# The attention output product of layer 2 as one level of Strassen, and the weight copies moved into layer 1's attention

## The reference

```
h  = rms_norm(x, norm_g);  u = h @ w_in
v_c, b_c, c_c, z_c, q, k, v, z_a, gate_logits = split(u)
y_c = b_c * causal_depthwise_conv(c_c * v_c, conv_w) * silu(z_c);   y_a = y_c @ w_conv_out
o   = sliding_window_attention(rms(q), rms(k), v, sinks) * silu(z_a);  y_b = o @ w_attn_out
g_a, g_b = split(sigmoid(gate_logits + gate_b))
out = x + (g_a * y_a + g_b * y_b) @ w_out
```

## Time and profile before

| | |
|---|---|
| median of three runs | 816.91 us |
| the profiled execution | 816.7 us |
| its span | 814.7 us |
| PE (matmul) busy | 99% |
| PEld (weight load) busy | 84% |
| DVE busy | 75% |
| ACT busy | 40% |
| POOL busy | 22% |
| piece 88, first of the attention output product, starts | 604.61 us |
| the gate stage starts | 691.65 us |

### The profile page before, as it was taken

How to read it: one execution, slowest core, us unless ns; L and a number is a source line. 1 busy time by engine, 2 the same in 40 slices (tenths; PEclk the granted TensorE clock), 3 DMA queues, 4 the chain that set the end, 5 groups by cost and what they waited for, 6 DMA issues and landing times.

```text
span 814.7 us, 11429 instructions
## 1 busy us (share of the span) xinstructions
PE 808.5 (99%) x4220; PEld 687.1 (84%) x4220; DVE 609.4 (75%) x1096; ACT 321.9 (40%) x701; POOL 182.6 (22%) x189
## 2 busy tenths in 40 slices
PE   9999999999999999999999999999999999999998
PEld 7778888888888888888888888888888888999986
DVE  4998778768984476885579788978952269599998
ACT  4374465632212255334445554441000122355580
POOL 2212111111111221121324445444323224000000
PEclk9999999999999999999999999999999999999999
DMA  7332214445143222653365555566876335866562
GB/s 239 87 97 77 79 52 153 158 157 179 53 155 126 82 83 77 208 175 90 91 130 130 125 119 120 128 130 155 168 165 158 104 88 145 233 182 183 182 205 78
DMA packets 129565, 108.92 MB, mean 134 GB/s; under 512 B 4525, under 2 KB 101350, under 8 KB 129510
## 3 DMA queue, kind: packets, MB, share of 16 engines
q1 hardware_dynamic: 123142, 95.60, 38.4%
q0 software_dynamic: 6336, 12.58, 9.4%
q10 hardware_dynamic: 32, 0.01, 0.0%
HBM read 106.08 MB, written 27.26 MB: 164 GB/s over the span
## 4 chain that ended last, share of the span: by engine, by line
PE 92%; DVE 5%; issue 1%; ACT 1%; DVEq 0%; ACTq 0%
PE proj L1736 24%; PE proj L1738 24%; PE proj L1737 24%; PE bank_t L1750 3%; PE bank_o L1825 2%; DVE x L1447 1%; DVE w_lo L1142 1%; PE score L1738 1%; PE score L1737 1%; PE score L1736 1%; PE score L1900 1%; PE score L1899 1%; PE score L1811 1%; PE score L1810 1%; PE bank_o L1918 1%
## 5 line engine op out<-in xcount | busy, mean ns | idle before, releaser
L723 POOL TENSOR_SCALAR w_hi<-w_raw 128x1024 fp32r<-128x1024 f32 x109 | 128.8, 1182 | 436.2 <-DMA w_raw<-in_w_in_dram 310.8
L1142 DVE TENSOR_TENSOR w_lo<-w_raw,w_hi 128x1024 fp32r<-128x1024 f32 x145 | 179.9, 1244 | 60.2 <-POOL w_hi L723 59.6
L1736 PE MATMUL proj<-xt_hi,w_hi 128*128 128x512 f32 (+1 forms) x448 | 171.1, 382 | 0.0
L1738 PE MATMUL proj<-xt_hi,w_lo 128*128 128x512 f32 (+1 forms) x448 | 168.1, 375 | 0.0
L1737 PE MATMUL proj<-xt_lo,w_hi 128*128 128x512 f32 (+1 forms) x448 | 167.8, 375 | 0.0
L1738 PEld LDWEIGHTS proj<-xt_hi,w_lo 128*128 128x128 f32 x448 | 84.4, 188 | 15.5
L1737 PEld LDWEIGHTS proj<-xt_lo,w_hi 128*128 128x128 f32 x448 | 84.5, 189 | 14.2
L1736 PEld LDWEIGHTS proj<-xt_hi,w_hi 128*128 128x128 f32 x448 | 84.5, 189 | 13.9
L1736 PE MATMUL proj<-w_hi,xt_hi 128*128 128x512 f32 x152 | 61.0, 401 | 0.2 <-ACT prob L922 0.2
L1738 PE MATMUL proj<-w_hi,xt_lo 128*128 128x512 f32 x152 | 59.5, 392 | 0.0
L1737 PE MATMUL proj<-w_lo,xt_hi 128*128 128x512 f32 x152 | 59.4, 391 | 0.0
(11 more groups left out here) (420 smaller groups left out, 1774.4 us busy)
## 6 DMA issues: line engine op xcount, KB each, us to landing
w_raw<-in_w_in_dram SPq DMA_DIRECT2D x79, 512.0 KB, 3.8
w_sums<-in_w_in_dram SPq DMA_DIRECT2D x8, 1024.0 KB, 7.5
w_raw<-w_sums SPq DMA_DIRECT2D x32, 256.0 KB, 3.3
w_raw<-in_w_out_dram SPq DMA_DIRECT2D x14, 512.0 KB, 3.3
w_raw<-in_w_in_dram SPq DMA_DIRECT2D x26, 256.0 KB, 3.6
w_sums<-w_sums POOLq DMA_DIRECT2D x6, 1024.0 KB, 9.9
w_sums<-in_w_out_dram SPq DMA_DIRECT2D x4, 1024.0 KB, 6.8
w_sums<-in_w_in_dram POOLq DMA_DIRECT2D x4, 1024.0 KB, 9.9
```

The lines of the kernel that those rows point to most:

```text
L723: pool.tensor_scalar(hi, raw, 1.0, 1.0, ALU.mult, ALU.mult).then_inc(hi_done, 1)
L1142: dve.tensor_tensor(lo, raw, hi.bitcast(F32), ALU.subtract).then_inc(w_split, 1)
L1736: pe.matmul(out, left[0], right[0], start=first, stop=False)
L1738: return pe.matmul(out, left[1], right[0], start=False, stop=last)
```

## The change

1. The attention output product becomes one level of Strassen in 14 pieces (`AOUT` = 88 to 101, `COUT` = 102 the first of the convolution's output product): seven block products for each of two column pairs. A piece is a weight block's 512 rows x 256 columns, 2 x 4 x 3 = 24 matmuls of 256 tokens, still in the ring of 4 slots.
2. A fourth group of `w_sums` (four copies, four gathers more). The 16 copies stand behind the loads of pieces 12 to 27; the 16 gathers at pieces 53, 55, 57, 59, 62, 64, 66, 68, 71, 73, 75, 77, 80, 82, 84, 86, the new group first. POOL waits for a group's copies, not for all.
3. `OS`: ACT rounds, DVE takes the low part, and for half of the chunks only 256 tokens. The factor 0.5 of the results moves into the gating (0.5 becomes 0.25).
4. Four sums of activations on DVE at pieces 85 to 87, rounded on ACT at 87 and 88, low parts on DVE at 88, 88, 89, 90. Results are combined on DVE (`combine_out`), for each pair seven additions of 512 numbers, in place of ACT's eight tiles.
5. The banks rotate over all eight; the first pieces behind wait for the last additions.

```diff
-U_AOUT = U_CONV + KC
-U_COUT = U_AOUT + KC // 4
+U_COUT = U_CONV + KC
+AOUT = 4 * U_COUT
+OUT_PIECES = 7 * 2
+COUT = AOUT + OUT_PIECES
+GATES = 4 * UNITS + OUT_PIECES
+OUT_ORDER = [A11, A12, A22, S2, S1, S4, S3]
+GROUPS = 4
+ATTENDED = 3
-COPY_AT = [*range(4 * U_GA, 4 * U_O0), *range(4 * U_Z0, 4 * U_Z1)]
-SUM_AT = [4 * U_Z1 + 4 + 3 * i for i in range(4 * GROUPS)]
+COPY_AT = range(4 * U_RQK, 4 * U_O0)
+GROUP_ORDER = [ATTENDED, 0, 1, 2]
+SUM_AT = [4 * U_Z1 + 1 + 9 * i // 4 for i in range(4 * GROUPS)]
+SO_SUM_AT = ((AOUT - 3, 1), (AOUT - 2, 0), (AOUT - 2, 1), (AOUT - 1, 0))
+SO_HI_AT = ((AOUT - 1, 0), (AOUT - 1, 1), (AOUT, 0), (AOUT, 1))
+SO_LOW_AT = ((AOUT, 0), (AOUT, 1), (AOUT + 1, 1), (AOUT + 2, 1))
...
+            if n < COUT:
+                pair, i = divmod(n - AOUT, 7)
+                return [right_of(ATTENDED, OUT_ORDER[i])[:, 256 * pair:256 * pair + 256].rearrange("(k p) c -> p k c", p=P)]
...
+        def out_bank(x):
+            return gate_banks[(x + SLOTS) % 8]
...
+                if n == AOUT:
+                    sp.wait_ge(w_gathered[ATTENDED], 16 * 4)
...
-                group, step = divmod(i, 4)
+                group, step = GROUP_ORDER[i // 4], i % 4
                 t = (0, 2, 1, 3)[step]
-                if i == 0:
-                    pool.wait_ge(w_copied, 16 * 4 * GROUPS)
+                if step == 0:
+                    pool.wait_ge(w_copied[group], 16 * 4)
                 if step >= 2:
                     pool.wait_ge(w_gathered[group], 16 * step)
...
+                        elif kind == "OS":
+                            act.wait_ge(o2_gated, WIN_STEPS)
+                            tokens = slice(0, 256 if m < 4 else S)
+                            act.activation(o2_hi[:, m, tokens], gT2[:, m, tokens], ACT.Copy).then_inc(o2_hi_done, 1)
...
+            def attended_sum(i):
+                x11, x12, x21, x22 = (quarter(gT2, row, col) for row in range(2) for col in range(2))
+                if i == 0:
+                    dve.wait_ge(o2_split, KC)
+                    dve.tensor_tensor(x22, x22, x21, ALU.subtract).then_inc(so_summed, 1)
...
+            def attended_low(i):
+                product = (S2, S1, S4, S3)[i]
+                dve.wait_ge(so_hi_done, i + 1)
+                hi, lo = sum_of_attended(product)
+                dve.tensor_tensor(lo, raw_sum(product), hi.bitcast(F32), ALU.subtract).then_inc(so_split, 1)
...
+            def combine_out(x):
+                pair, i = divmod(x, 7)
+                product = OUT_ORDER[i]
+                if product in (A11, A22):
+                    return
+                psum, kept = out_bank(x), out_bank(7 * pair + OUT_ORDER.index(A22))
+                dve.wait_ge(piece_done, AOUT + x + 1)
...
+                elif product == S3:
+                    dve.scalar_tensor_tensor(out=out(1, 1), in0=v_sum_out, scalar=-1.0, in1=psum, op0=ALU.mult, op1=ALU.subtract).then_inc(out_combined, 1)
+                    dve.tensor_tensor(w_sum, w_sum, psum, ALU.add).then_inc(out_combined, 1)
+                    dve.wait_ge(out_combined, 7 * pair + 6)
+                    dve.tensor_tensor(out(1, 0), w_sum, kept, ALU.add).then_inc(out_combined, 1)
...
+                    if half == 1 and AOUT <= n < COUT:
+                        combine_out(n - AOUT)
...
+            def attended_product(x):
+                n = AOUT + x
+                product = OUT_ORDER[x % 7]
+                wait_low(n)
...
+                else:
+                    wait_combined_out(x - 8)
+                if x < 7 and LEFT[product][0]:
+                    pe.wait_ge(so_split, (S2, S1, S4, S3).index(product) + 1)
+                left = left_of_attended(product)
+                w = [ring_parts(n, i)[0] for i in (1, 2)]
+                for j in range(2):
+                    for k in range(4):
+                        last = products(out_bank(x)[:, j, :], [t[:, k, j * P:(j + 1) * P] for t in w], [t[:, k, :] for t in left], k == 0, k == 3)
+                last.then_inc(piece_done, 1)
...
                         if u == U_COUT:
                             pe.wait_ge(yc_done, KC)
+                            wait_combined_out(8 + q)
```

More of the change, by code:

```diff
@@ L127, in unit_columns @@
             (TRA, [("w_in_2", Z2 + 512 + P * j) for j in range(4)])][u]
-    if u < U_AOUT:
+    if u < U_COUT:
         t = u - U_CONV
         return TRA, [("w_in_2", c + P * t) for c in (CV, CC, CB, CZ)]
-    t = 4 * ((u - U_AOUT) % (KC // 4))
-    return TRA, [("w_attn_out_2" if u < U_COUT else "w_conv_out_2", P * (t + j)) for j in range(4)]
+    return TRA, [("w_conv_out_2", P * (4 * (u - U_COUT) + j)) for j in range(4)]
 UNIT = [unit_columns(u) for u in range(UNITS)]
@@ L446, in left_of, with sum_of_attended, left_of_attended @@
             return [t[:, chunk:chunk + 4, token:token + 256] for t in ((hi, lo), (s_hi, s_lo))[source]]
+        def sum_of_attended(product):
+            place = {S2: 0, S1: 1, S4: 2}
+            if product == S3:
+                return [quarter(t, 1, 0) for t in (o2_hi, o2_lo)]
+            return [t[:, 4 * place[product]:4 * place[product] + 4, :] for t in (so_hi, so_lo)]
+        def left_of_attended(product):
+            source, chunk, token = LEFT[product]
+            if source:
+                return sum_of_attended(product)
+            return [t[:, chunk:chunk + 4, token:token + 256] for t in (o2_hi, o2_lo)]
         def pair_of(t, c, r):
@@ L846, in take_first, with take_first_out @@
                 act.activation(u_sum, gate_banks[7 * c % 8], ACT.Copy).then_inc(u_copied, 1)
+            def take_first_out(pair):
+                act.wait_ge(yc_done, KC)
+                if pair:
+                    act.wait_ge(out_combined, COMBINED[S2])
+                act.wait_ge(piece_done, AOUT + 7 * pair + 1)
+                act.activation(u_sum, out_bank(7 * pair), ACT.Copy).then_inc(out_first, 1)
             def take_tanh(c, r):
@@ L963, in _ @@
                         else:
[L965 to L968, removed]
+                            if u >= U_COUT:
+                                t = 4 * (u - U_COUT) + j
+                                act.wait_ge(out_combined, OUT_PIECES)
+                                act.activation(part[:, t, :], b, ACT.Copy, scale=0.5).then_inc(evacuated[j], 1)
                                 continue
-                            if u > U_CONV and last_tanh[0] < U_AOUT and last_tanh[0] >= U_CONV:
+                            if u > U_CONV and last_tanh[0] < U_COUT and last_tanh[0] >= U_CONV:
                                 act.wait_ge(yc_done, u - U_CONV)
@@ L983, in _ @@
                         gate_step(n - GATES)
-                    if half == 1 and 4 * U_COUT + 2 <= n < 4 * U_COUT + 6:
-                        q = n - 4 * U_COUT - 2
+                    if (n, half) in SO_HI_AT:
+                        product, after_sums = ((S2, 3), (S1, 1), (S4, 4), (S3, 2))[SO_HI_AT.index((n, half))]
+                        act.wait_ge(so_summed, after_sums)
+                        act.activation(sum_of_attended(product)[0], raw_sum(product), ACT.Copy).then_inc(so_hi_done, 1)
+                    if half == 1 and AOUT <= n < COUT:
+                        if (n - AOUT) % 7 == 0:
+                            take_first_out((n - AOUT) // 7)
+                    if half == 1 and COUT + 2 <= n < COUT + 6:
+                        q = n - COUT - 2
                         act.wait_ge(sx_summed, (4, 6, 8, 10)[q])
@@ L1691, in _ @@
                         left_lows(c)
-                    if half == 1 and 0 <= n - 4 * U_COUT < 5:
-                        input_sums(n - 4 * U_COUT)
-                    if half == 1 and 0 <= n - 4 * U_COUT - 3 < 4:
-                        input_low(n - 4 * U_COUT - 3)
+                    if half == 1 and AOUT <= n < COUT:
+                        combine_out(n - AOUT)
+                    if half == 1 and 0 <= n - COUT < 5:
+                        input_sums(n - COUT)
+                    if half == 1 and 0 <= n - COUT - 3 < 4:
+                        input_low(n - COUT - 3)
                     if n >= FINAL and (n - FINAL) % 2:
@@ L1717, in _ @@
                         take_tiles(n, half)
-                    if half == 1 and WIN_FIRST <= n < 4 * U_AOUT and not splits_wait(n, half):
+                    if half == 1 and WIN_FIRST <= n < AOUT and not splits_wait(n, half):
                         for m in ROUNDED_AT[n]:
                             split_piece(m)
+                    if (n, half) in SO_LOW_AT:
+                        attended_low(SO_LOW_AT.index((n, half)))
+                    if (n, half) in SO_SUM_AT:
+                        attended_sum(SO_SUM_AT.index((n, half)))
                     if (n, half) == (0, 0):
```

127 lines of the change are left out of this document (90 added, 37 removed).

## The result

The changed kernel takes 819.1 us (median; 817.9 to 821.0), the kernel before on the same chip 817.0 (816.2 to 817.8): ratio 1.0027, 95% interval 1.0019 to 1.0035, slower by 0.27%. The profiled run took 818.0 us, 1.3 more than the profiled run of before; its span of 816.2 is 1.57 us over the span of before.

What follows compares the result with a forecast made beforehand. PE, busy 808.5 of 814.7 us, was taken as the bound. -3.20 + 5.0 + 0.25 + 0.1 = +2.15 us on the profiled 816.7 gave 818.9, as the median 819.1 us; range 813.8 to 821.8.

Steps and rivals of the forecast that it cites:

- the second rival: Attention output product: the stall only eats the gain, stop 3.4 us, 817.5 us; with stops of 1.6 to 4.4, chance 0.27.
- the forecast: Likeliest case: a stop of 4.4 to 6 us in the attention output product, 818.5 to 820.2 us, chance 0.4.
- Term 1: Attention output product itself: 14 pieces of 2.88 us, 40.32 us instead of 43.52, a gain of 3.20 us.
- Term 3: Attention output product: weight loads held behind late accumulating copies make PE stand once, 5.0 us, before piece 92.
- the upper case: Attention output product: copies of 12.1 us each, or the load of piece 89 held too, give a 6.2 us stop.
- the forecast's own case: Load of piece 92, held behind the last accumulating copy, lands at 618.6 and stops PE for 5.0 us.
- Term 2: Four-slot weight ring at 2.88 us a piece: the shorter cover still suffices, cost 0, bounds 0 to 2 us.
- the sums of term 4: DVE's four activation sums before piece 90: cost 0 thanks to DVE's idle time; without it 4.9 us would delay piece 90.
- term 4: Small edges: piece 103's bank 0.25 us, copies behind pieces 12 to 27 0.1, moved rounding and window attention masks 0.
- The clock: Half clock behind the stall in the attention output product: counted as 0, with +2.9 us kept for the range.
- the first: Rival for the attention output product: loads are not held, PE never stands, 814.1 us, chance 0.2.

Runs made afterwards that it cites:

- e7: Kernel before with only the change's data movement (16 copies, 16 accumulating copies), its attention output product as it was: 817.3 us, ratio 0.9997.
- e9: Changed kernel with accumulating copies behind pieces 52, 54, ... 82 and DVE's four sums two to three half pieces earlier: 816.0 us, ratio 0.9985.
- e10: e9 with its last accumulating copy moved from behind piece 82 to behind piece 87: 819.3 us, ratio 1.0022.
- e5: Changed kernel with its 16 accumulating copies behind pieces 48, 50, ... 78: 819.3 us, ratio 1.0026.
- e6: e5 with DVE's four sums also two to three half pieces earlier: 818.8 us, ratio 1.0021.
- e12: e9 with ScalarE instead of POOL rounding weight pieces 91 to 101: 815.4 us, ratio 0.9979.
- e2: Changed kernel with only DVE's four sums moved two to three half pieces earlier: 818.9 us, ratio 1.0018.
- e4: Changed kernel with PE streaming 22 idle matmuls before it waits for the low half of piece 90: 818.7 us, ratio 1.0017.
- e8: e6 with six PE waits forced by ScalarE copies, before pieces 97 to 109; ran once, stops of 1.11 to 5.23 us, whole time not given.
- e11: e9 with ScalarE's casts and DVE's low halves of the four sums one half to two half pieces earlier: 817.1 us, ratio 1.0001.

## Why the prediction came out as it did

The median was forecast to the tenth (819.1) and the sign is right, but the tenth is luck: two wrong sizes cancelled, and the profiled run, forecast at 818.9, took 818.0. Half of the working is wrong. The sign that the prediction set itself, one stop of 4 to 6 us before the fourth or fifth product, was not met: the stop was 2.81 us, before the third. By its stop the run belongs to the second rival (1.6 to 4.4), by its time to the forecast.

- **Term 1 (-3.20): right.** 0.12 apart, 336 times, 40.32 us.
- **Term 3 (+5.0 at piece 92): right in kind, wrong in place, size and path.** A load held behind a late accumulating copy is at the head of PE's stop (e7, e9 and e10 show it from three sides). But it was the load of 89, which the text gave as the upper case, and it reached PE one piece later, through DVE's row: DVE waited for POOL's rounding at piece 89, and the stop before 90 came from the order of DVE's program. The stop was 2.81, not 6.2. The 6.2 doesn't come out of the prediction's rows: copies of 12.1 give 5.4 by the same chain. The copies took 10.1 and 10.2 us, not 11.9, so the last one landed at 614.7, not at 617.3. The load of 92, the forecast's own case, landed at 615.7; alone it would have cost some 1.8 us instead of 5.0, an estimate from that landing, 1.05 and 1.22 of work and PE's 616.2. Its lateness fell into the first stop.
- **Term 2 (0) and the sums of term 4 (0): wrong.** The prediction itself said that without DVE's idle time the sums would delay piece 90, and then counted the idle time as safe; the load of 89 took it. Even with no load of the stage held, 1.0 us of stop remains before 90 (e5) and 0.7 to 1.4 later (e5, e6, e9). One reason shown is that in my walk every subtraction of DVE took 1.22 us, while one that meets POOL's rounding takes up to 2.06; that this alone makes the stops is not shown (e12).
- **The clock (0, up to 2.9): wrong.** It cost 1.6 in the profile of after, behind a stop of 2.81, little more than half of the one forecast. The Trainium skill ("TensorE: Matmul & The Clock Gate", section "HAM oscillation — how this bites in real kernels") had warned that a wait for a DMA can put TensorE back to half rate, and the trace agrees: granted clock 0.57 right behind the stop.
- **The rest of term 4: right as far as shown.** No new wait before 600 us; the conv output starts 45.0 us after piece 88, as forecast, out of other parts; e7's median is that of before. But only in this trace is the product just 0.06 us later than before. In the traces of e2, e4, e7 and e9 to e12 it starts 0.4 to 1.1 us later, with no wait above 0.3 us; the kernel before has one trace, so whether that is the copies or scatter stays open. Piece 103's wait was 0.05 (forecast 0.25), though 0.8 to 1.1 in e2, e4 and e10.
- **A reading:** of the three waits of the earlier trace rows, the last one (0.2 us) lies between 20 and 60 us and not in the first microseconds. Nothing rests on it.
- **The sum:** forecast 5.0 (stop) + 0.25 (piece 103) + 0.1 (ahead) = 5.35; measured 2.81 (stop) + 1.6 (clock) + 0.27 (piece 94, in no term) + 0.05 (piece 103) + 0.06 (ahead) = 4.8. A stop forecast too long by 2.2 made up for a clock counted at nothing. The medians differ by 2.1, 0.6 more than the two spans, so other runs lose more than the traced one.
- **Rivals:** loads are held, so the first falls as a description of this kernel; as a condition (no load of the stage held) the nearest is e6, which keeps 2.4 of the 3.2 us in the stage and loses them ahead of it, and then e9, which keeps 1.35.

Open: what decides within the scatter of 3 us from run to run. The clock has a part in it: the three runs of the changed kernel with a mean granted clock of 0.999 or 1.000 took 817.9 to 818.1 us, the ten with 0.995 to 0.998 took 818.0 to 821.0. What makes the clock fall in one run and not in the next is not shown. The edge below is a candidate, since issue times differ by some tenths between runs, but only profiled runs show which load was held.

## What to carry to other kernels

When a stage is made of shorter pieces, the time from load to use shrinks with them, and every transfer and every in-order row that used to fit under it must be counted again; a shorter stream of PE is worth only what its slowest supplier leaves. Put bulk copies where nothing but a deep buffer depends on loads, and end them one landing time before the loads of the tight stage and of what stands ahead of it in the same in-order row. Where an engine's idle time is the cover, ask which late input would use it up before PE does.

## What the runs showed of the hardware

- **An edge at half a microsecond.** Over all 14 traces, up to 640 us: of 22 weight loads issued from 0.3 us ahead to 0.42 us behind an accumulating copy, 21 landed after 3.5 to 4.0 us (one 5.96), some 5 to 8 us before the copy. All 80 issued 0.51 to 2 us behind took 7.8 to 11.0 (no load fell between 0.42 and 0.51). The 38 issued 2 to 4 us behind took 6.7 to 9.4 and landed 1.0 to 1.8 after the copy. A few tenths of a microsecond in SyncE's or POOL's program so decide over 5 us of a load. Why the edge lies there is not shown.
- **DVE and POOL hold each other up.** A 128x1024 subtraction of DVE of 1.22 us takes up to 2.06 where it meets POOL's rounding, and that takes up to 2.1 instead of 1.05; beside ScalarE's rounding DVE keeps 1.22 (e12). In e9's rows above the subtraction of 612.71 kept its 1.21 us and POOL's rounding of 612.93 took 1.91; the subtractions of 613.84 and 615.83 took 2.06 and ended 1.06 and 1.08 us after POOL's had. The Trainium skill ("SBUF — State Buffer", section "SBUF: two separate sides") says that the engine that loses the shared port pair stands until the other has done; these rows agree.
- **The clock behind short stops.** PE fell to 1.2 GHz behind stops of 2.32 (e10), 2.81 (after) and 2.9 to 5.2 us (e8), and not behind 1.1 to 2.2 (e8, e11) and 2.61 (e2). So the length of a stop alone does not decide it: 2.32 us brought a fall and 2.61 none. The price was 1.6 to 3.0 us on top of the stop.
